# One PSUM bank with a fence for the mixers' products, split mLSTM reads, and other places for the attention norms

## The reference

```python
def _mlstm_scan(q, k, v, li, lf):            # one direction; called again on flipped inputs
    ...
    dmat = jnp.where(mask, b[..., :, None] - b[..., None, :] + li[..., None, :], -jnp.inf)
    m_inter = b + m_prev[..., None]
    m_l = jnp.maximum(jnp.max(dmat, axis=-1), m_inter)
    wq = jnp.exp(dmat - m_l[..., None]) * jnp.einsum('bclhd,bcshd->bhcls', qc, kc)
    sc = jnp.exp(m_inter - m_l)
    num = jnp.einsum('bhcls,bcshd->bclhd', wq, vc) + jnp.einsum('bclhd,bched,bhcl->bclhe', qc, c_prev, sc)
    den = jnp.sum(wq, axis=-1) + jnp.einsum('bclhd,bchd,bhcl->bhcl', qc, n_prev, sc)
    den = jnp.maximum(jnp.abs(den), jnp.exp(-m_l)).transpose(0, 2, 3, 1)
    return (num / den[..., None]).reshape(Bsz, S, H, Dh)

def _trunk(x, ...):
    for l in range(DEPTH):                   # DEPTH = 2
        h = _rmsnorm(x, mix_norm[l])
        aq, ak, av, sz, sxbc, sdt, mq, mk, mv, mo, mi, mf = jnp.split(h @ w_in[l], offsets, axis=-1)
        ya = _window_attention(...)          # rms norm of q and k, window 128, sink
        yb = _ssd_mixer(...)                 # both directions, chunks of 128
        yc = _mlstm_mixer(...)               # both directions, head norm, sigmoid gate
        x = x + jnp.concatenate([ya, yb, yc], axis=-1) @ w_out[l]
        x = x + _expert_choice_ffn(_rmsnorm(x, ffn_norm[l]), router[l], w_gate[l], w_up[l], w_down[l])
    return x
```

## Time and profile before

| | us |
|---|---|
| median of 3 executions | 2582.53 |
| lowest and highest | 2578.44 and 2583.72 |
| the profiled execution | 2578.44 |
| its span, first to last instruction | 2576.8 |
| PE busy | 2388.8 |
| VectorE busy | 1057.4 |
| ScalarE busy | 556.7 |
| GpSimd busy | 527.9 |

### The profile page before, as it was taken

How to read it: one execution, slowest core, us unless ns; L and a number is a source line. 1 busy time by engine, 2 the same in 40 slices (tenths; PEclk the granted TensorE clock), 3 DMA queues, 4 the chain that set the end, 5 groups by cost and what they waited for, 6 DMA issues and landing times. The chain is left out here.

```text
span 2576.8 us, 34177 instructions
## 1 busy us (share of the span) xinstructions
PE 2388.8 (93%) x13486; PEld 1730.0 (67%) x13486; DVE 1057.4 (41%) x2034; ACT 556.7 (22%) x1194; POOL 527.9 (20%) x544
## 2 busy tenths in 40 slices
PE   5999998999995999999969999999899959999997
PEld 3567577874553788788735675878655538878876
DVE  3662355486537111111138514445864471111111
ACT  3220223243320011111132203323433201111110
POOL 1002443133210121111110114432331101111111
PEclk8999999999997999999989999999999979999999
DMA  6010222121226587887331021211211276788782
GB/s 217 19 34 17 98 82 82 58 91 50 74 74 228 201 283 264 292 285 250 116 128 36 17 64 67 98 50 66 83 59 69 80 259 213 262 288 288 249 290 68
DMA packets 149654, 357.61 MB, mean 139 GB/s; under 512 B 9981, under 2 KB 38273, under 8 KB 149410
## 3 DMA queue, kind: packets, MB, share of 16 engines
q1 hardware_dynamic: 134514, 313.42, 34.1%
q0 software_dynamic: 14976, 41.95, 6.5%
HBM read 313.06 MB, written 47.52 MB: 140 GB/s over the span
## 5 line engine op out<-in xcount | busy, mean ns | idle before, releaser
L1469 PE MATMUL ps<-MID,HT 128*128 128x512 f32 (+1 forms) x2176 | 595.1, 495 | 4.3 <-PE ps L1469 3.1
L1469 PE MATMUL ps<-HT,MID 128*128 128x160 f32 (+1 forms) x4192 | 582.3, 306 | 8.1 <-DVE HT L975 3.8
L1469 PEld LDWEIGHTS ps<-HT,MID 128*128 128x128 f32 (+1 forms) x4192 | 562.8, 189 | 25.9 <-issue 25.7
L1469 PE MATMUL ps<-RING,HT 128*128 128x256 f32 (+2 forms) x2080 | 473.4, 396 | 9.0 <-ACT MID L791 4.3
L1469 PEld LDWEIGHTS ps<-RING,HT 128*128 128x128 f32 (+1 forms) x2080 | 375.5, 192 | 97.4 <-issue 43.6
L1469 PEld LDWEIGHTS ps<-MID,HT 128*128 128x128 f32 (+1 forms) x2176 | 231.5, 152 | 225.7 <-issue 209.2
L1469 PE MATMUL ps<-HT,RING 128*128 128x512 f32 (+1 forms) x960 | 352.8, 524 | 3.1 <-ACT MID L785 2.4
L984 DVE SCALAR_TENSOR_TENSOR HT<-HT,ps 128x160 f32<-128x160 f32 x128 | 41.1, 321 | 711.7 <-ACT HT L961 711.7
L1469 PEld LDWEIGHTS ps<-HT,RING 128*128 128x128 f32 x960 | 180.4, 191 | 162.7 <-issue 155.0
L741 POOL DMA_INDIRECT y_sample<-SCR,idxs x32 | 50.6, 1581 | 741.1 <-ACT SCR L968 741.1
L975 DVE TENSOR_TENSOR HT<-ps,part 128x512 f32<-128x512 f32 (+1 forms) x220 | 141.5, 643 | 119.0 <-PE ps L1809 52.8
(11 more groups left out here) (217 smaller groups left out, 2167.2 us busy)
## 6 DMA issues: line engine op xcount, KB each, us to landing
MID<-w_gate SPq DMA_DIRECT2D x32, 2048.0 KB
MID<-w_up SPq DMA_DIRECT2D x32, 2048.0 KB
MID<-w_down SPq DMA_DIRECT2D x32, 2048.0 KB, 14.7
RING<-w_in SPq DMA_DIRECT2D x22, 1024.0 KB, 5.3
SCR<-cs_rows SPq DMA_DIRECT2D x20, 1024.0 KB, 5.3
SCR<-m_rows SPq DMA_DIRECT2D x20, 512.0 KB, 4.0
MID<-y_sample SPq DMA_DIRECT2D x16, 512.0 KB, 7.8
MID<-w_out SPq DMA_DIRECT2D x8, 1024.0 KB, 6.4
```

What stands on the lines that cost most here:

```text
L1469: return pe.matmul(out, a, b, start=start, stop=stop)
```

## The change

It has four parts. PE's products go to one bank: `ssd_products` and `ml_products` write to one bank each, one half of the array's rows after the other, with a `fence` between the halves, which makes PE wait until the matmul ahead of it is complete. `ml_sum` also takes one half after the other for its second part. `ml_read` and `ml_output` handle the two directions by separate instructions. The squares and roots of the attention norm for blocks 4 to 7 are in chunks 5 to 8 of the mLSTM loop, those of 8 and 9 in the hand-written stretch. There `attn_norm(4)` stands behind the last head norm on GpSimd, and `attn_den(2)` ahead of `keep_turned(4)` on VectorE. The wait of `turn_qk(0)` for `mw_made` is gone, since bank 3 has no other reader.

```diff
@@ -416,6 +416,7 @@
         topt_made = layer_sem("topt_made")
         g_copied = layer_sem("g_copied")
         quad_spread = layer_sem("quad_spread")
+        pe_fence = layer_sem("pe_fence")
         rng = range(min(x.num for x in layer_sems), max(x.num for x in layer_sems) + 1)
         assert len(rng) == len(layer_sems)
 
@@ -687,23 +688,23 @@
                         attn_norm(2)
                         attn_norm(3)
                         attn_scale(0)
-                        attn_root(4)
-                        attn_norm(4)
                     if c >= 1:
                         pool.wait_ge(h_summed, c)
                         rroot(rsb, ssb, MH, 4.0 / HD, 4 * EPS, h_rooted)
-                    if 1 <= c <= 4:
+                    if 1 <= c < NC - 1:
                         attn_root(c - 1)
                     if c in (3, 4):
                         attn_norm(c - 3)
 
+                attn_norm(4)
                 attn_scale(1)
+                attn_root(NC - 2)
+                attn_root(NC - 1)
                 for n in range(NC + 1):
                     if n >= 1:
                         pool.wait_ge(n2_squared, n)
                         rroot(rsb, ssb, 1, 1.0 / D, EPS, n2_rooted)
                     if n + 5 < NC:
-                        attn_root(n + 5)
                         attn_norm(n + 5)
                     if n + 2 < NC:
                         attn_scale(n + 2)
@@ -1138,9 +1139,10 @@
                 def ssd_weights(c):
                     dve.wait_ge(cb_made, c + 1)
                     dve.wait_ge(d_summed, c + 1)
+                    cb = ps[:, 4, 0:256].rearrange("p (g t) -> p g t", g=2)
                     for g in range(2):
                         v = DM[:, c % 2, 0, g * 512:(g + 1) * 512].rearrange("p (h t) -> p h t", h=4)
-                        tt(v, v, ps[:, 4 - g, 0:P].unsqueeze(1).to_broadcast([P, 4, P]), ALU.mult, w_made)
+                        tt(v, v, cb[:, g, :].unsqueeze(1).to_broadcast([P, 4, P]), ALU.mult, w_made)
 
                 def ssd_output(c):
                     dve.wait_ge(y_made, c + 1)
@@ -1197,38 +1199,40 @@
                     dve.wait_ge(st_made, c + 1)
                     for d in range(2):
                         dve.wait_ge(md_exp, 2 * c + d + 1)
-                        v = DMM[:, c % 2, d].rearrange("p (j q) t -> p q j t", q=2)
-                        tt(v, v, ps[:, 2:4, 0:2 * P].rearrange("p q (j t) -> p q j t", j=2), ALU.mult, mw_made)
-
-                nd = TMP[:, 0:520]
-                hsd = SCR[:, 3392:3904]
-                hs, hd = hsd[:, 0:256], hsd[:, 256:512]
-                inter = TMP[:, 520:1040]
+                        tt(DMM[:, c % 2, d], DMM[:, c % 2, d], quarter(2), ALU.mult, mw_made)
+
+                nd = [heads(TMP[:, 260 * d:260 * d + 260], 4) for d in range(2)]
+                hs, hd = heads(SCR[:, 3392:3648], 4), heads(SCR[:, 3648:3904], 4)
+                t4 = heads(TMP[:, 520:780], 4)
 
                 def ml_read(c):
 
                     dve.wait_ge(nd_made, c + 1)
-                    tt(inter.rearrange("p (m q e) -> p q m e", q=2, e=65), ps[:, 4:8:3, 0:260].rearrange("p q (m e) -> p q m e", m=4),
-                       SC[:, c].rearrange("p d n -> p (d n)").rearrange("p (m q) -> p q m", q=2).unsqueeze(3).to_broadcast([P, 2, 4, 65]),
-                       ALU.mult)
-                    tt(nd.rearrange("p (d n) -> p d n", d=2), ps[:, 5:7, 0:260], inter.rearrange("p (d n) -> p d n", d=2), ALU.add, nd_read)
+                    for d in range(2):
+
+                        tt(t4.rearrange("p (j q) e -> p q j e", q=2),
+                           ps[:, 4:8:3, 130 * d:130 * d + 130].rearrange("p q (j e) -> p q j e", j=2),
+                           SC[:, c, d, :].rearrange("p (j q) -> p q j", q=2).unsqueeze(3).to_broadcast([P, 2, 2, 65]), ALU.mult)
+                        tt(nd[d], heads(ps[:, 5 + d, 0:260], 4), t4, ALU.add, nd_read)
 
                 def ml_output(c):
-
-                    raw = heads(nd, 8)[:, :, HD:HD + 1].rearrange("p h e -> p (h e)")
-                    stt(den, raw, -1.0, raw, ALU.mult, ALU.max)
-                    tt(den, den, EML[:, c].rearrange("p d n -> p (d n)"), ALU.max)
+                    for d in range(2):
+                        dn = den[:, 4 * d:4 * d + 4]
+                        raw = nd[d][:, :, HD:HD + 1].rearrange("p h e -> p (h e)")
+                        stt(dn, raw, -1.0, raw, ALU.mult, ALU.max)
+                        tt(dn, dn, EML[:, c, d, :], ALU.max)
                     link(dve.reciprocal(rec, den))
-                    tt(heads(hsd, 8), heads(nd, 8)[:, :, 0:HD], wide(rec, HD), ALU.mult)
+                    for d in range(2):
+                        tt(hd if d else hs, nd[d][:, :, 0:HD], wide(rec[:, 4 * d:4 * d + 4], HD), ALU.mult)
                     tt(hs, hs, hd, ALU.add)
                     tt(hd, hs, hs, ALU.mult)
-                    link(dve.tensor_reduce(out=ssb[:, 0:4], in_=heads(hd, 4), axis=AX, op=ALU.add), h_summed)
+                    link(dve.tensor_reduce(out=ssb[:, 0:4], in_=hd, axis=AX, op=ALU.add), h_summed)
 
                 def ml_gate(c):
                     dve.wait_ge(h_rooted, c + 1)
-                    tt(heads(hs, 4), heads(hs, 4), wide(rsb[:, 0:4], HD), ALU.mult)
+                    tt(hs, hs, wide(rsb[:, 0:4], HD), ALU.mult)
                     dve.wait_ge(o_tanh, c + 1)
-                    stt(O[:, c, :], OTH[c % 2], 1.0, hs, ALU.add, ALU.mult, h_done)
+                    stt(O[:, c, :], OTH[c % 2], 1.0, SCR[:, 3392:3648], ALU.add, ALU.mult, h_done)
 
                 def attn_square(n):
 
@@ -1304,10 +1308,10 @@
                 attn_den(0)
                 attn_shift(1, 1)
                 keep_turned(3)
-                attn_square(4)
                 ml_output(NC - 1)
                 attn_den(1)
-                attn_square(5)
+                attn_square(NC - 2)
+                attn_square(NC - 1)
                 attn_shift(2, 0)
                 keep_y(0, 2)
                 ml_gate(NC - 1)
@@ -1354,10 +1358,9 @@
                 keep_y(1, 0)
                 take_x(0)
                 keep_y(1, 1)
+                attn_den(2)
                 keep_turned(4)
                 keep_y(1, 2)
-                attn_square(6)
-                attn_den(2)
                 for n in range(1, NC - 1):
                     add_x(n - 1, 1)
                     if n + 4 < NC:
@@ -1374,8 +1377,6 @@
                     if n + 2 < NC:
                         attn_den(n + 2)
                     keep_y(n + 1, 2)
-                    if n + 6 < NC:
-                        attn_square(n + 6)
                     route_shift(n - 1)
                     route(n - 1)
 
@@ -1465,6 +1466,8 @@
 
             @block.tensor
             def _(pe):
+                fence = counter(pe, pe_fence)
+
                 def mm(out, a, b, start=True, stop=True):
                     return pe.matmul(out, a, b, start=start, stop=stop)
 
@@ -1630,9 +1633,8 @@
                     if c >= 1:
                         pe.wait_ge(w_made, 2 * c)
 
-                    for g in range(2):
-                        last = mm(ps[:, 4 - g, 0:P], BC[64 * g:64 * g + 64, 0, t:t + P], BC[64 * g:64 * g + 64, 1, t:t + P])
-                    last.then_inc(cb_made, 1)
+                    fence(mm(ps[:, 4, 0:P], BC[0:64, 0, t:t + P], BC[0:64, 1, t:t + P]))
+                    mm(ps[:, 4, P:2 * P], BC[64:P, 0, t:t + P], BC[64:P, 1, t:t + P]).then_inc(cb_made, 1)
 
                 def ssd_sum(c):
                     t = tcol(c)
@@ -1697,31 +1699,30 @@
                 def ml_products(c):
                     if c >= 1:
                         pe.wait_ge(mw_made, 2 * c)
-                    for h in range(MH):
+                    for h in (0, 2, 1, 3):
+                        if h == 1:
+                            fence(last)
                         b = 64 * (h % 2)
-                        last = mm(ps[:, 2 + h % 2, h // 2 * P:(h // 2 + 1) * P], QK[b:b + 64, 2 + h // 2, c * P:(c + 1) * P],
+                        last = mm(ps[:, 2, h * P:(h + 1) * P], QK[b:b + 64, 2 + h // 2, c * P:(c + 1) * P],
                                   QK[b:b + 64, h // 2, c * P:(c + 1) * P])
                     last.then_inc(st_made, 1)
 
                 def ml_sum(c):
                     pe.wait_ge(mw_made, 2 * c + 2)
                     if c >= 1:
-                        pe.wait_ge(nd_read, c)
+                        pe.wait_ge(nd_read, 2 * c)
                     for d in range(2):
                         for h in range(MH):
                             mm(ps[:, 5 + d, 65 * h:65 * h + 65], DMM[:, c % 2, d, h, :], V[:, c, h, :])
-                    for j in range(2):
+                    for h in (0, 2, 1, 3):
+                        b = 64 * (h % 2)
                         for d in range(2):
-                            for q in range(2):
-                                b = 64 * q
```

(8 more changed lines are left out.)

## The result

The changed kernel takes 2620.18 us (median of 4 executions, 2619.34 to 2621.25), the kernel before 2580.49 (4 executions, 2577.34 to 2583.72). The ratio is 1.0154, 95% interval [1.0137, 1.0172]: slower by 39.7 us. The forecast was 2617, with a range of 2602 to 2633.

What follows compares the result with a forecast made beforehand. PE was taken to bound most stages, VectorE the mLSTM chunks with a square. Terms 7.9 + 1.0 + 2.0 + 1.4 + 5.9 + 0.3 = 18.5 us a layer, 37.0 for two, gave 2617 us; range 2602 to 2633.

Steps and rivals of the forecast that it cites:

- 1 and 2, VectorE in the loop: mLSTM loop: split instructions add 0.95 us a chunk; with moved squares +7.9, then +1.0 to the first scores, a layer.
- 3, TensorE: mLSTM loop: fence and one-half order raise PE's chunk from 7.26 to 8.9 us, hidden under VectorE's 9.05 to 9.2.
- steps 4 and 5: mLSTM loop entry delayed by slower products and sum, +2.0; SSD products' fences paid in three chunks, +1.4 us a layer.
- The rival in which weight loads no longer overlap: mLSTM loop: PE's chunk becomes 12.5 us, 59 us more over both layers, 2676 us; chance 0.02.
- 6, the denominators: Before turn_y(1,2): new VectorE wait +3.7, later wait removed -0.7, half clock behind the gap +2.9; 5.9 us a layer.
- 7, the rest: Transition to attention +0.3 us a layer; turn_qk(0) wait and the output projection's lost squares and roots 0.
- The rival on the faster side: Output projection held by VectorE and GpSimd; losing four squares with roots gains 11 us a layer, 2566 us; chance 0.03.
- PE binds the loop: mLSTM loop: dearer fence or serial passes make the period 9.8 instead of 9.2 us, +8, 2625 us; chance 0.13.
- The den wait costs little: Before turn_y(1,2): ScalarE ready earlier or clock holds, so the wait costs 0 to 1 us a layer, 2606; chance 0.14.
- The change does nothing that matters: Fences find PE drained, squares fill VectorE's waits; only split instructions cost, 17 us in all, 2595 us; chance 0.06.

Runs made afterwards that it cites:

- e10: Kernel before with the split reads and the moved squares together, TensorE and the order of attn_den(2) untouched: ratio 1.0072.
- e9: Changed kernel with attn_den(2) put back behind keep_turned(4) and keep_y(1, 2): ratio 1.0115 to the kernel before.
- e6: Kernel before with only the SSD products in one bank with a fence: ratio 1.0019, 4.8 us.
- e1: Kernel before with only attn_den(2) moved ahead of keep_turned(4) on VectorE: 2590.85 us against 2582.27, ratio 1.0030.
- e3: Kernel before with only the squares and roots moved, blocks 4 to 7 to chunks 5 to 8, 8 and 9 to the hand-written stretch: ratio 1.0001.
- e2: Kernel before with only ml_read and ml_output handling the two directions by separate instructions: ratio 1.0042, 10.8 us.
- e7: Kernel before with only the mLSTM products in one bank, one row half at a time, with a fence: ratio 1.0013.
- e8: Kernel before with only the inter-chunk products of ml_sum in the new order, one row half after the other, no fence: ratio 1.0013.
- e4: Kernel before with the whole TensorE part: SSD and mLSTM products in one bank with fences, and the new inter-chunk order: ratio 1.0084.

## Why the prediction was right, point by point

The total was forecast at 37.0 us above before and came out at 39.7 (2617 against 2620.18 us). The reason given for it holds too: with all parts present VectorE sets the pace of the mLSTM loop, and PE mostly runs beneath it. It holds with three sizes off, and a part of the closeness is luck: the TensorE part measures 4.8 us more than its terms and the denominators 1.7 less, each +- 6.

**1 and 2, VectorE in the loop: right.** The prices of the split (0.46 a read instruction, 0.20 a small one, 0.46 for each half product) are those of the trace of after, and e10, which has these two steps alone, costs 18.6 us against 18.4. What made the forecast work here is that the two steps were priced together, chunk by chunk. Apart they are worth 10.8 and 0, since each of them alone finds waits in the later chunks that it can fill.

**3, TensorE: sizes nearly right, the cover thinner than forecast.** The products cost +0.77 (forecast 0.72), the inter-chunk order +0.49 (forecast 0.9, taken from full-height passes; 16 passes took 1.53, not 1.93), so a chunk takes 8.52 and not 8.9. At full clock it is hidden, as said. But the cover of 0.5 us counts only at 2.4 GHz. With a stretch at 1.2 GHz in it a chunk took 11.82 us and VectorE waited for it. The change and e9 have the same loop. Between reads 1 and 8 VectorE waited for PE four times in their traces, 0.32, 0.77, 1.71 and 1.12 us, each time for the first sum behind a half-clock stretch and nowhere else; behind two more such stretches in e9 it did not wait.

The forecast had priced the clock only behind turn_y(1,2), and nowhere in the loop. This is the step that was mis-sized. The TensorE part as a whole adds 11.6 us +- 6 in the changed kernel, where steps 4 and 5 said 6.8. That the clock makes up the difference is what the traces suggest (in the trace of the change layer 1 lost 10.5 us in the loop and 4.1 behind it, layer 0 9.4 and 1.3, with 2.5 and 0.3 us of these waits in the loops; in e9 the two loops took 65.73 and 65.32 us). No run took the clock away, so how much of the 11.6 us it is stays open.

**The rival in which weight loads no longer overlap** fell. Sixteen passes of 65 columns, eight in a row in the same row half, took 1.53 us, 0.096 each, while the page after lists the loads of its group at a mean of 0.181 (0.197 for those of 64 rows and 128 columns alone). The Trainium skill, "TensorE: Matmul & The Clock Gate", Part 3 under "The mechanism", says that a load overlaps only when the row groups differ; this row and the earlier trace rows don't agree with it for fp32 here. The order is not free either: the same passes in alternating halves took 0.065 each.

**4 and 5, entry and SSD: right in place and about in size.** The entry cost 1.6 and 2.0 (2.0 forecast). The SSD loop cost 1.4 and 2.6 (1.4 forecast), e6 2.4 a layer. The weights stay 16.32 us apart.

**6, the denominators: right in every link of its chain, a little dear.** The gap was forecast at 4.8 us and is 4.94, and the wait at turn_p(2,0) went. The clock was mis-sized: the forecast took 2.9 us from the gap at 588.53 (half of the 6.5 us that it names would be 3.25). In layer 0 the work behind the new gap lost 1.30 in turn_y(1,2) and 0.08 in the next group, 1.4 in all, and in layer 1 about 2.5 (6.59 us from turn_y(1,2) at 1931.35 to the scores at 1937.94, 4.05 before). e1 lost as much in layer 0 (6.57). Measured as a whole it is 7.7 us alone (interval 4.9 to 10.6) and 10.1 +- 6 in the changed kernel, against 11.8.

**7, the rest: right.** The output projection gained nothing that shows from losing four squares: e3 is 1.0001 in all with 0.8 us more in the loop of layer 0, and the window behind the change is as full as before. The rival on the faster side had 11 us a layer for them.

**The rivals.** *PE binds the loop* is what happened for single chunks, mostly in layer 1, and by another cause than the one named: not a dearer fence, but a half-clock stretch ahead of the wait. *The den wait costs little* did not happen: 4.94 us stand in the trace. *The change does nothing that matters* would have been 2595, with only the splits paid; e2, which has only them, is at 2593, and the change is 25 us above the 2595.

## What to carry to other kernels

When two engines run a loop nearly in step, price all edits of a loop together and per chunk, and take the larger engine. Edits on one side cost little until the sum crosses the other side, so tests of one edit at a time give numbers that don't compose: e7 and e8 were 0.13% each and 0.64% together, while e4's 0.84% shrank to 0.45% beside a slower VectorE (difference 0.39 +- 0.28). That the four parts added up to the whole was an accident of two such effects of opposite sign (e10 is above the sum of its parts), and only the runs that leave one part out or join two showed it. A cover of a few tenths of a microsecond on PE should be computed at both clock levels.
